# Another order of allocation for the on-chip buffers of a two-layer hybrid transformer block

## The reference

```
a_b, a_c, a_u, q, k, v, r_g, r_u, d_v, d_g, gl = _split_cols(h @ w_in)
ys = (_short_conv(a_b, a_c, a_u, conv_a) @ w_a_out, y_b @ w_b_out,
      (jax.nn.gelu(r_g) * rec) @ w_c_out,
      _conformer_conv(d_v, d_g, conv_d, conv_d_b, ln_d_g, ln_d_b) @ w_d_out)
out = sum_n sigmoid(gl_n) * ys_n @ w_out
x = x + gt1 * out
x = x + gt2 * ((silu(gate) * up) @ w_ffn_out)      # gate, up = modulated(x) @ w_ffn_in
```

## The kernel before

| buffer | before | after | buffer | before | after |
|---|---|---|---|---|---|
| HH | 128 | 0 | S / SR | 384 | 128 |
| HL | 256 | 0 | TMP / TMPR | 224 | 128 |
| ZH, ZL | 384 | 0 | CD | 256 | 128 |
| WH, WL | 224 | 0 | RAW | 224 | 128 |
| X | 128 | 0 | G | 384 | 128 |
| PADA / PADR | 256 | 0 | CST | 352 | 96 |

## Time and profile before

### The profile page before, as it was taken

How to read it: one execution, slowest core, us unless ns; L and a number is a source line. 1 busy time by engine, 2 the same in 40 slices (tenths; PEclk the granted TensorE clock), 3 DMA queues, 4 the chain that set the end, 5 groups by cost and what they waited for, 6 DMA issues and landing times.

```text
span 1977.6 us, 29316 instructions
## 1 busy us (share of the span) xinstructions
PE 1951.1 (99%) x11006; PEld 1664.1 (84%) x11006; DVE 1414.0 (72%) x2475; ACT 909.4 (46%) x1439; POOL 811.2 (41%) x353
## 2 busy tenths in 40 slices
PE   7999999999999999999999999999999999999998
PEld 5778888888888778878788887777899999999998
DVE  5896666667788868788885544589788878645555
ACT  5787544232222242245222212589955434565444
POOL 1002322334343443444344443400646887454442
PEclk9999999999999999999999999999999999999999
DMA  8222211222323235533544452312433555445553
GB/s 343 83 86 78 93 65 60 74 101 85 106 85 106 86 128 200 204 139 117 228 176 187 177 213 88 144 66 84 149 107 132 188 189 190 176 174 184 178 189 128
DMA packets 38701, 276.25 MB, mean 140 GB/s; under 512 B 4416, under 2 KB 4416, under 8 KB 6336
## 3 DMA queue, kind: packets, MB, share of 16 engines
q1 hardware_dynamic: 38592, 274.77, 38.0%
HBM read 273.70 MB, written 1.05 MB: 139 GB/s over the span
## 4 chain that ended last, share of the span: by engine, by line
PE 87%; DVE 7%; ACT 3%; issue 1%; DMA 1%; POOL 1%; SPq 0%; DVEq 0%; POOLq 0%; ACTq 0%
PE PS L592 86%; DVE PS L1545 1%; ACT WH L1023 1%; DMA CD<-in_modw 1%; PE PS L905 1%; POOL WL L535 1%; DVE TMP L1548 1%; DVE PS L1542 1%; DVE SM L1991 0%; ACT PS L1023 0%; DVE ZL L1545 0%; DVE SM L1548 0%; ACT HH L1023 0%; DVE HL L1545 0%; DVE X L1545 0%
## 5 line engine op out<-in xcount | busy, mean ns | idle before, releaser
L535 POOL TENSOR_TENSOR WL<-RAW,WH 128x1024 fp32r<-128x1024 f32 (+1 forms) x337 | 802.1, 2399 | 1142.6 <-ACT WH L1023 1142.6
L1023 ACT ACTIVATE WH<-RAW 128x1024 fp32r<-128x1024 f32 (+1 forms) x416 | 414.6, 1043 | 619.9 <-PE PS L592 567.6
L592 PE MATMUL PS<-HH,WH 128*128 128x512 f32 (+2 forms) x1968 | 682.9, 347 | 4.1 <-issue 1.8
L592 PE MATMUL PS<-HH,WL 128*128 128x512 f32 (+2 forms) x1968 | 672.7, 342 | 0.0
L592 PE MATMUL PS<-HL,WH 128*128 128x512 f32 (+2 forms) x1968 | 669.9, 341 | 0.3 <-DVE HL L1545 0.2
L592 PE MATMUL PS<-ZH,WH 128*128 128x512 f32 (+1 forms) x1312 | 444.6, 339 | 3.4 <-DVE HL L1542 2.6
L592 PE MATMUL PS<-ZH,WL 128*128 128x512 f32 (+1 forms) x1312 | 443.9, 339 | 0.0
L592 PE MATMUL PS<-ZL,WH 128*128 128x512 f32 (+1 forms) x1312 | 441.8, 339 | 0.0
L592 PEld LDWEIGHTS PS<-HH,WH 128*128 128x128 f32 x1968 | 370.0, 188 | 57.3 <-issue 8.3
L592 PEld LDWEIGHTS PS<-HL,WH 128*128 128x128 f32 x1968 | 371.1, 189 | 50.9 <-issue 3.8
L592 PEld LDWEIGHTS PS<-HH,WL 128*128 128x128 f32 x1968 | 370.3, 188 | 45.7
(11 more groups left out here) (210 smaller groups left out, 1735.9 us busy)
## 6 DMA issues: line engine op xcount, KB each, us to landing
RAW<-in_stream SPq DMA_DIRECT2D x200, 1024.0 KB, 4.8
CD<-in_modw SPq DMA_DIRECT2D x22, 1024.0 KB, 7.0
G<-in_modw SPq DMA_DIRECT2D x22, 1024.0 KB, 7.0
RAW<-in_stream SPq DMA_DIRECT2D x8, 768.0 KB, 4.2
CD<-in_lruw SPq DMA_DIRECT2D x2, 2048.0 KB, 11.1
X<-in_xT SPq DMA_DIRECT2D x2, 1024.0 KB, 7.9
S<-in_modw SPq DMA_DIRECT2D x2, 1024.0 KB, 13.8
RAW<-in_modw SPq DMA_DIRECT2D x1, 1024.0 KB, 20.3
```

The lines of the kernel that those rows point to most:

```text
L535: nc.gpsimd.tensor_tensor(WL[:, a:b], RAW[:, a:b], WH[:, a:b].bitcast(F32), ALU.subtract)\
L592: return nc.tensor.matmul(out, lhs, rhs, start=start, stop=stop)
L1023: return nc.scalar.activation(out, in_, f, **kw)
```

## The change

The buffers are allocated in another order. `MOD` (384 bytes) comes first, then `X`, the weights' and inputs' parts, with three small buffers set between `HH` and `HL`, and then the others. No size, no instruction, no access within a buffer, no wait and no transfer is different; only the byte at which each buffer begins.

```diff
+        MOD = sb("MOD", 2 * 48)
         X = sb("X", KC * NT)
-        HH = sb("HH", KC * UROW, F32R)
-        HL = sb("HL", KC * UROW, F32R)
+        WH = sb("WH", 2 * SLAB, F32R)
+        WL = sb("WL", 2 * SLAB, F32R)
         ZH = sb("ZH", KC * NT, F32R)
         ZL = sb("ZL", KC * NT, F32R)
+        HH = sb("HH", KC * UROW, F32R)
+        AMP = sb("AMP", 2 * 2 * KC)
+        SELB = sb("SELB", 32)
+        LC = sb("LC", 2 * 16)
+        HL = sb("HL", KC * UROW, F32R)
         S, SR = sb_and_rounded("S", KC * NT)
+        CD = sb("CD", KC * NT)
+        RAW = sb("RAW", 2 * SLAB)
+        TMP, TMPR = sb_and_rounded("TMP", 7 * NT)
         G = sb("G", KC * GW)
-        CD = sb("CD", KC * NT)
         PADA, PADR = sb_and_rounded("PADA", 2 * GW)
-        RAW = sb("RAW", 2 * SLAB)
-        WH = sb("WH", 2 * SLAB, F32R)
-        WL = sb("WL", 2 * SLAB, F32R)
-        TMP, TMPR = sb_and_rounded("TMP", 7 * NT)
         PRM = sb("PRM", DEPTH * NPRM)
         ROPE = sb("ROPE", 2 * NX)
         CST = sb("CST", 5 * P + 2)
-        MOD = sb("MOD", 2 * 48)
-        AMP = sb("AMP", 2 * 2 * KC)
         CIN = sb("CIN", 2 * KC)
         SILC = sb("SILC", 32 * KC + 30)
-        SELB = sb("SELB", 32)
         SG = sb("SG", 2 * KC)
-        LC = sb("LC", 2 * 16)
         LT = sb("LT", 5 * 16)
```

## The result

The changed kernel takes 1960.55 us (median of 4 runs, 1958.75 to 1961.24) against 1982.48 of the kernel before beside it. The ratio is 0.9894, with a 95% interval of 0.9882 to 0.9906: 1.1% faster. The forecast was 1970 in a range of 1952 to 1992. The profiled execution has a span of 1958.7 us, 18.9 less than before.

The account below looks back on a forecast made before the run. TensorE was taken as the bound. Savings of 3.2 (H), 5.9 (Z), 3.2 (256 columns) and 1.4 us (value projection) sum to 13.7, 0.87 of it, 11.9, at the end: 1970 us, range 1952 to 1992.

Parts of the forecast that it names:

- terms for 512 columns: 512-column products on TensorE: H 3.2 us less (6.4 if every slow triple goes), Z 5.9 us less.
- The bound: Whole kernel: TensorE, busy 1951.1 of 1977.6 us, sets the time; 0.87 of any saving per matmul reaches the end.
- The mechanism: Main matmuls: how a moving row lies to the stationary block loaded during its stream changes; differences become multiples of 512 bytes.
- The price: 512-column matmuls after the change: mean 393 ns, taken from attention scores at 394, 393 and 391 ns.
- the quick rate: 512-column H products in 545 to 585 us: one matmul per 231 ns, 1178 ns in sum per triple.
- The slow rate: 512-column H products in 177 to 217 us: one per 234 ns, 1193 per triple; half of slow triples expected to stay.
- The 256-column term: 256-column H and Z products: 0.7 ns less per matmul, 3.2 us saved, with ends 0 and 7 us.
- The value projection: Where weights are what streams: mean falls from 288 to 280.7 ns, 1.4 us saved.
- Other engines at nothing: ScalarE, VectorE and GpSimd (ACT, DVE, POOL): buffer starts cost them nothing.
- That nothing changes: Rival: buffer starts do not set the matmul rates, only perhaps a stage's starting phase; 1982 us; chance 0.20.
- The collision: Rival: stream and next block's load conflict at equal places, quick 512-column streams become slow; 1992 us, or 2018; chance 0.20.
- The whole surplus: Rival: rounded 512-column products fall from 231 to at most 215 ns; 1879 us; larger gain up to this has 0.10.

Follow-up runs that it names:

- the last experiment: Changed kernel with WH and WL 192 bytes longer, weights 192 bytes in until the second layer's q, then at their start: 1948.95 us, ratio 0.9842.

## Why the prediction was right, and where its sizes were off

The direction and the wide range (1952 to 1992) held, but the forecast's own range, 1962 to 1975, was missed by 1.5 us, and the gain of 21.9 us is past the 8 to 20 that had been given 0.50. Both terms for 512 columns measured more than their stated ends: 15.6 us against 6.4 in H, 12.5 against 5.9 in Z. What follows names the step that was off.

**The bound** was right: with 21.1 us off TensorE's busy time, 18.9 went from the span, 0.90 against the 0.87 that I took. The agreement is no proof of the way in which 0.87 was found, the chain's share: the chain after has 81% of TensorE, and the last experiment, which starts from there, brought 0.64 of its saving to the end.

**The mechanism** was right: what counts is how a moving row lies to the stationary blocks. I had taken 512 bytes as the period from the change; the runs show 256. Shown: the kernel with all at 128 keeps the gain, each one-sided shift loses it, the old order with equal places has it. That it is the block loaded beside the stream, and not the stream's own, rests on the one run with WL alone displaced, which leaves 5 ns unexplained. Why the chip behaves so no run shows.

**The price** of a 512-column matmul after was the step that was mis-sized. I took 393 ns from the attention scores, because they are at a difference of zero, and that made the quick rate of the kernel before, 231 ns, the least that there could be. The main products came to a third rate, 226.7. The scores had 394, 393 and 391 ns and have 395, 392 and 393 after. Where they stand, the main products are slower too: in 225 to 345 us, where heads come between the products, HL,WH and HH,WL have 391 and 392 ns after the change, and the scores 391 to 393, against 389 for the same products in `a_cu`. The trace after shows how: from the start of a run at 60.5 us the first nine distances are 224 to 236 ns, mean 231, and only then 226 and 227 to the end of the run. So a run of a few matmuls between other shapes is no sample of a long run. (The third score product is also not at zero each time: in 9 of 32 cases the block loaded beside it is one of WH.) So H gave 15.6 us, not 3.2, and Z 12.5, not 5.9.

**The slow rate** was expected to stay for half its triples. It is gone: 177 to 217 us, where it ruled, now holds 178 matmuls, within one of `a_cu`. It had also been read too low: by the starts the slow rate is 235.5 ns, since two matmuls, not one, were begun before that stretch, so the two rates lay 4.4 and not 3 ns apart. Nor did the kernel before keep a rate for a whole stage, as I had put it: it changed at 643 us, inside `a_b`, at a pause.

**The 256-column term** had the wrong sign: 9.2 us lost for 3.2 gained. The score rows (280 and 281) were again the reason. The errors partly cancel: 13.7 us forecast on TensorE and 18.9 by the means. That the sum came so near is in part luck.

**The value projection**, 1.4 us forecast, gave 0.2: its first group went from 294 to 295, and the other two from 286 and 284 to 283. The sign set for it, near 281, did not come.

**Other engines at nothing** held, ACT at 908.0 for 909.4 us, DVE at 1416.5 for 1414.0, and POOL at 812.0 for 811.2.

**The rivals.** That nothing changes is refuted by the interval, and so is the Trainium skill's rule that PE never waits on anyone ("SBUF — State Buffer", "Who interferes with whom"), as far as it is read as "the place of a buffer costs nothing"; whether the surplus is a wait at a port no run here can show. The collision is refuted for 512 columns; for 256 the time goes its way by some 2 ns, and equal places are, with +96, the dearest of the differences tried, but that a collision is the cause is not shown. One reading that spoke for it was wrong: HH is not the quickest moving operand of a slow triple, since HH,WL, with the same rows, has the longest mean, 403. The whole surplus did not go: 226.7 ns is still 13 over the 213 of the prediction.

## What to carry to other kernels

Where TensorE is the bound and streams long rows in float32r with a new stationary block each time, work out the byte at which the moving rows and the stationary blocks begin, take the difference modulo 256, and try zero and 64 either side; it costs a reordering of allocations and gave 1.1% here, and 1.6% with a difference for each width. The best place depends on the width of the rows: zero for 512 columns, 64 either side for 256. Read the result as starts per stretch, since TensorE is busy 99% of the span either way. Do not take the rate of a short group between other shapes for that of a long one.

## What the runs showed of the hardware

At a difference of zero the distance between starts is 226.7 ns for 512 columns in the long stretches of the changed kernel, and 229 to 230 in 220 to 360 us, where attention products come between; it is 120.0 for 256 columns. At -128, -64, -32, +32 and +96 it is 232 to 233 for 512 columns, at +16 it is 231.6 and at +64 some 229 (the means of H and Z in the traces of those kernels). At -64 it is 113.3 or 117.8 for 256.

At one set of addresses more than one rate exists (231.1 and 235.5 ns before, in the stretches of the earlier trace rows; 113.3 and 117.8 in the last experiment). The changes from one to the other that were followed, one before and four in the last experiment, all fell on a pause of TensorE, and not each pause brought one. At a difference of zero a run of 512 columns can need some nine matmuls until it has its 226.7 ns.
